# The order of work at the last output product of a mixer block, and spare TensorE products in front of the first products behind two fused norms

## The reference, cut to what matters

```python
def modulate(x, shift, scale):
    return layer_norm(x) * (1 + scale) + shift

def post_norm(x, y, gate, g, b):
    return layer_norm(ALPHA * x + gate * y) * g + b
...
xn = rms_norm(h, g_mix)
proj = xn @ w_in
```

## Time and profile before

| | |
|---|---|
| Median of 3 runs | 2158.62 us (2153.17 to 2158.88) |
| Profiled execution, its own time | 2158.39 us |
| Its span in the trace | 2156.4 us |
| TensorE matmul busy | 2076.0 us (96%) |
| VectorE, ScalarE, GpSimd busy | 1161.5, 882.7, 790.1 us |
| TensorE clock granted over the span | 0.98 |

### The profile page before, as it was taken

How to read it: one execution, slowest core, us unless ns; L and a number is a source line. 1 busy time by engine, 2 the same in 40 slices (tenths; PEclk the granted TensorE clock), 3 DMA queues, 4 the chain that set the end, 5 groups by cost and what they waited for, 6 DMA issues and landing times. The chain is left out here.

```text
span 2156.4 us, 25771 instructions
## 1 busy us (share of the span) xinstructions
PE 2076.0 (96%) x10262; PEld 1605.7 (74%) x10262; DVE 1161.5 (54%) x2012; ACT 882.7 (41%) x1391; POOL 790.1 (37%) x405
## 2 busy tenths in 40 slices
PE   6999988999999899999999999989999999999999
PEld 3877667888887767667888887677776788888866
DVE  5366748996574579964522131345997553122124
ACT  4543334443332566863322222335667432222132
POOL 0243104676563324420544444001434134444420
PEclk9999999999999799999999999999999999999999
DMA  9134611323222202112333322221111133332212
GB/s 313 59 98 156 215 59 59 98 98 117 78 97 86 79 1 79 40 59 78 108 98 98 98 98 78 79 85 40 59 59 40 59 98 108 98 98 84 97 54 98
DMA packets 186662, 194.23 MB, mean 90 GB/s; under 512 B 8496, under 2 KB 181936, under 8 KB 186160
## 3 DMA queue, kind: packets, MB, share of 16 engines
q1 hardware_dynamic: 184880, 187.35, 27.1%
q10 hardware_dynamic: 1664, 5.24, 0.7%
HBM read 190.48 MB, written 2.10 MB: 89 GB/s over the span
## 5 line engine op out<-in xcount | busy, mean ns | idle before, releaser
L2773 POOL TENSOR_TENSOR wl<-ring,wh 128x1024 fp32r<-128x1024 f32 (+1 forms) x253 | 621.3, 2460 | 908.5 <-ACT wh L1421 907.6
L1421 ACT ACTIVATE wh<-ring 128x1024 fp32r<-128x1024 f32 (+2 forms) x294 | 304.4, 1043 | 352.3 <-PE ps L796 265.2
L794 PE MATMUL ps<-xh,wh 128*128 128x512 f32 x960 | 377.0, 393 | 1.9 <-POOL wl L2773 1.7
L796 PE MATMUL ps<-xh,wl 128*128 128x512 f32 x960 | 374.3, 390 | 0.0
L795 PE MATMUL ps<-xl,wh 128*128 128x512 f32 x960 | 374.3, 390 | 0.0
L794 PE MATMUL ps<-acts,wh 128*128 128x512 f32 x880 | 348.7, 396 | 3.1 <-DVE wl L1950 3.1
L796 PE MATMUL ps<-acts,wl 128*128 128x512 f32 x880 | 350.5, 398 | 0.0
L795 PE MATMUL ps<-acts,wh 128*128 128x512 f32 x880 | 347.5, 395 | 0.0
L2415 DVE SCALAR_TENSOR_TENSOR mix<-ps,par,mix 128x441 f32<-128x441 f32 (+2 forms) x352 | 213.6, 690 | 34.0 <-ACT mix L1651 33.9
L794 PEld LDWEIGHTS ps<-xh,wh 128*128 128x128 f32 x960 | 180.6, 188 | 45.5 <-issue 7.8
L796 PEld LDWEIGHTS ps<-xh,wl 128*128 128x128 f32 x960 | 180.5, 188 | 38.0
(11 more groups left out here) (429 smaller groups left out, 3133.0 us busy)
## 6 DMA issues: line engine op xcount, KB each, us to landing
ring<-in_w_ff_dram SPq DMA_DIRECT2D x64, 1024.0 KB, 5.3
ring<-in_w_in_dram SPq DMA_DIRECT2D x28, 1024.0 KB, 5.2
ring<-in_ffn_w_up_dram SPq DMA_DIRECT2D x22, 1024.0 KB, 5.0
ring<-in_w_ada_dram SPq DMA_DIRECT2D x17, 1024.0 KB, 5.1
ring<-in_w_out_dram SPq DMA_DIRECT2D x12, 1024.0 KB, 5.3
ring<-in_ffn_w_down_dram SPq DMA_DIRECT2D x8, 1024.0 KB, 5.1
ring<-in_w_ple_gate_dram SPq DMA_DIRECT2D x8, 1024.0 KB, 5.2
early<-in_w_ada_dram SPq DMA_DIRECT2D x7, 1024.0 KB, 12.1
```

Source lines behind the costliest of these rows:

```text
L794: t.matmul(b[0:m, 0:n], s.hi[:, k, a:a + m], x2[0][:, k, :], start=k == ks[0], stop=False)
L796: i = t.matmul(b[0:m, 0:n], s.lo[:, k, a:a + m], x2[0][:, k, :], start=False, stop=k == ks[-1])
L1421: a.activation(s.hi[:, :, c], s.ap[:, :, c], ACT.Copy).then_inc(*up("hi", "hi", name, hf))
L2773: p.tensor_tensor(s.lo[:, :, c], s.ap[:, :, c], s.hi[:, :, c].bitcast(F32), ALU.subtract).then_inc(*up("lo_pool", "lo", name, hf))
```

## The change

It is made in three places. (1) At the last output product, `ahead_of_norm` on ScalarE squares rows 4 and 5, then does the high halves, then squares rows 6 and 7; before, row 6 came ahead of the high halves. This function is also used for `p2`, whose last product has no halves to do. (2) The half of weights that the plan gives to `("ug", 0, 0)` moves: ScalarE rounds it before `statistics` instead of behind it, and its low part is made by VectorE before `statistics` instead of by GpSimd behind `centered`. (3) A function `spin` issues matmuls of plain float32, 128x128 by 128x512, on constants, into a PSUM bank that the first real product starts afresh: 4 ahead of the rows behind `p1`, 7 ahead of the rows behind `p2`. Nothing reads them.

```diff
@@ tensor
+            def spin(b, n):
+
+                for i in range(n):
+                    t.matmul(b[:, :], ones, con[:, 0:512], start=True, stop=True)
+
...
                     for key in first:
-                        use(key, (key[0], 0, 0), (key[2],), who="pool")
+                        use(key, (key[0], 0, 0), (key[2],), who="vec" if key == first[0] else "pool")
                         take(key, keep=True)
+                    spin(ps(first[0]), 4)
                     for k in range(8):
                         e.wait_ge(*at("xl", "f", k))
@@ layer_mixer (called with spin as a further argument)
                         for key, w in first:
                             use(key, s.name, (0, 1), key[3] == 3, 0)
                             take(key, where=w)
+                        spin(ps(first[0][0]), 7)
                         for hf in range(2):
                             e.wait_ge(*at("lo", s.name, hf))
@@ scalar, ahead_of_norm
                 if j in (6, 7):
-                    for n in ((0, 1, 2, 3), (4, 5, 6))[j - 6]:
+                    for n in ((0, 1, 2, 3), (4, 5))[j - 6]:
                         square(tag, n, mix[:, n, :], sqf, at("shifted", tag, n))
                 if j == 7:
                     high()
+                    square(tag, 6, mix[:, 6, :], sqf, at("shifted", tag, 6))
                     square(tag, 7, mix[:, 7, :], sqf, taken(("mean", tag)))
@@ scalar
             ahead_of_norm("p1", 7, lambda: high(("wout", 7)))
+            high(("ug", 0, 0))
             statistics("p1")
-            high(("ug", 0, 0))
@@ vector
+            low(("ug", 0, 0))
             statistics("p1", True)
@@ vector, up1
-                    low(("ug", g, jl))
+                    if (g, jl) != (0, 0):
+                        low(("ug", g, jl))
```

More of the change, by code:

```diff
@@ L1166, in tensor @@
                 n = layers[l]
-                layer_mixer(e, t, l, part, product_t, turn, take, fold, spread, use)
+                layer_mixer(e, t, l, part, product_t, turn, take, fold, spread, use, spin)
                 for j in range(8):
@@ L1231, in tensor, with layer_mixer @@
                     banks.drop(("parts", "g1"))
-        def layer_mixer(e, t, l, part, product_t, turn, take, fold, spread, use):
+        def layer_mixer(e, t, l, part, product_t, turn, take, fold, spread, use, spin):
             n = layers[l]
```

## The result

The changed kernel takes 2145.5 us in the median of 5 runs (2142.68 to 2150.59), beside 2158.62 for the kernel before in 5 runs (2153.17 to 2158.94). The ratio is 0.9942 with an interval of 0.9921 to 0.9963, a gain of 12.5 us within 8.0 to 17.1. The forecast was 2143, range 2137 to 2151.

What follows compares the result with a forecast made beforehand. TensorE was taken to set the time, with waits behind `p1` and `p2`. Gains of 14.4 and 1.5 us sum to 15.9, less 0.4 for a clock fall, from 2158.4 to 2143 us; range 2137 to 2151.

Steps and rivals of the forecast that it cites:

- The sums: Sums of `p1`: with the new order, ScalarE's copy comes 3.37 us after the last product, as behind `p2`; 5.7 us gained.
- The half ahead of `statistics` at no cost: Ahead of `statistics` at `p1`: the moved half delays ScalarE's copy by 0 to 0.5 us, taken as 0; VectorE's part is covered.
- The chain of statistics: Behind `p1`, from copy to VectorE's first row: 5.43 us as behind `p2`, in place of 7.32; rows start 7.63 us earlier.
- VectorE's eight rows: Behind `p1`: 23.73 us in place of 24.71, 0.98 off one `xl` slowed beside GpSimd's half; last row at 335.77.
- the rule that the forecast weighed: VectorE's two-SBUF-input operation is blocked until a GpSimd one reading SBUF ends; in `p1` rows it would add 0.3 us gain.
- TensorE behind `p1`: The 96 matmuls keep up with VectorE at full clock and end one row after the last `xl`, at 338.56; gain 14.4 us.
- The spares behind `p1`: Four spare products end by 316.7, ahead of the first `xl` at 317.37; they cost nothing and hold TensorE's clock.
- first rival: The clock falls all the same: `p1` rows begin at half clock for 5.3 us, 3.2 us less gain, 2146.5; chance 0.17.
- second price: Same clock fall hitting the spare products too: they end at 319.0 and 719.3, rows at 343.2 and 733; 2155 us.
- The spares behind `p2`: Seven spares, 6.0 us at full clock, end 0.5 us after the first row is ready; delay absorbed, gain 1.5 us.
- The middle and the rest: From 356 to 700 us the `p1` gain is not given back; half-clock stretches elsewhere are worth 2 to 4 us either way.
- the last one: Rival at both places: spare products do nothing, the order does all, `p2` stays as it is; 2144.5 us, chance 0.05.

Runs made afterwards that it cites:

- squares alone: Kernel before with only square 6 moved behind the two high halves; the weight half stays behind `statistics` on GpSimd, no spare products: 2152.72 us, ratio 0.9986.
- change again: The changed kernel profiled and timed once more with nothing altered, against the kernel before: ratio 0.9947; its profiled run took 2147.87 us.
- spares alone: Kernel before plus 4 spare products behind `p1` and 7 behind `p2`, old order kept: 2158.19 us, ratio 0.9997.
- order alone: Changed kernel without both calls of `spin`, so both moves of order and no spare products: 2147.31 us, ratio 0.9952 against the kernel before.
- fill: Changed kernel plus 128-column spare products inside the statistics (3 and 2), with 4 and 4, 4 and 5, or no spares ahead of rows: ratios 0.9947, 0.9946, 0.9949.
- doubled spares: Changed kernel with 8 and 14 spare products in place of 4 and 7: 2156.47 us, ratio 0.9989 against the kernel before.

## Why the prediction was right, and what it had wrong

The forecast of 2143 us stands 2.5 below the median, inside its range. Point by point:

- **The sums.** Forecast: 3.37 us from the end of the product to the copy, priced by `p2`. Measured 3.37 or 3.38 in each kernel with the new order. Right, and the squares alone show that it is their order that does it.
- **The half ahead of `statistics` at no cost.** Forecast 0 to 0.5. The copy followed at 3.37 with the half and without it (squares alone). Right. VectorE's low half of 1.22 us (311.63) ended ahead of its next step at 313.59.
- **The chain of statistics.** Forecast 5.43 us from copy to first row, at full clock. The change again has 8.94 - 3.37 = 5.57, right; the first profile of the change has 9.63 - 3.37 = 6.26, since the clock fell inside the spread there. The change is not safe from that.
- **VectorE's eight rows.** Forecast 23.73; measured from 318.04 to 340.03 + 1.63 = 341.66, 23.62. Right. What is won is 24.71 - 23.62 = 1.09, where the forecast had taken 0.98 off. The third `xl` of 1.86 us is gone, and it is there again in the squares alone, which leave the half on GpSimd. By the rule that the forecast weighed (the Trainium skill, SBUF — State Buffer, "Who interferes with whom") the `xl` beside GpSimd's `centered` should be held up too. The forecast took the 0.88 us in the earlier trace rows to speak against that. It doesn't, and the traces bear the rule out for both. GpSimd and VectorE, first in the change, then in the spares alone:

```profile
324.50 1.29 POOL L2830 TENSOR_TENSOR mix<-mix,arena_f 128x512 f32<-128x512 f32 x1
```

```profile
324.09 1.27 POOL L2827 TENSOR_TENSOR mix<-mix,arena_f 128x512 f32<-128x512 f32 x1
324.34 1.57 DVE L2371 SCALAR_TENSOR_TENSOR xl<-mix,mod,xh 128x512 fp32r<-128x512 f32 x1
```

  In the change GpSimd's instruction ends at 325.79, and the `xl` of 325.54 at 326.34, 0.55 us behind it. In the spares alone the ends are 325.36 and 325.91, 0.55 again; with the half, in the earlier trace rows, 331.39 and 331.94, once more 0.55. It is so for all 29 `xl` of the thirteen profiles that start well inside a GpSimd instruction. An `xl` takes 1.86, 1.57 or 0.80 us by how much of GpSimd's instruction is still to come, and beside `centered` that happened to be little.
- **TensorE behind `p1`: the step that failed.** The forecast let TensorE end "one row after the last `xl`", 338.56 or 35.3 us after the product. Measured at full clock: 37.11 + 0.23 = 37.3, although the last `xl` ends where it was forecast (32.55 us after the product, forecast 32.53). The last two `xl` come one directly behind the other (340.03, two in 1.63 us; the same is in the earlier trace rows), so that the last row at which TensorE waits for VectorE is row 6 (it starts at 340.84), and row 7 only comes behind it. It is two rows of 2.7 us behind the last `xl` but one, not one behind the last: 2.0 us of 14.4 that the forecast's own rows could have shown. The gain there was 12.3 us in the change again and 11.7 in the first profile.
- **The spares behind `p1`.** Forecast: hidden, and holding the clock. They are hidden (they end 0.45 or 1.4 us ahead of the first `xl`), the clock stays at 1.00 in the rows, and it is worth 1.1 us rather than the 3.2 of the first rival. That rival priced the half clock by TensorE's own work over 5.3 us. It lasted 4.0 us in the rows and put the second row 2.1 us back, and about half of that was made up, since VectorE paces the rows. (With the doubled spares of its second price the four would end at 313.28 + 6.88 = 320.2 and not at 319.0; nothing hangs on it.)
- **The spares behind `p2`: mis-sized.** Forecast 6.0 us of spares ending 0.5 us behind the first row, and 1.5 us won. They took 7.38 and 7.08 us in the two profiles of the change, the first real matmul started 1.8 us behind the first `xl`, and 0.4 us was won. The working took the full clock for granted between the spread and the rows; the clock had fallen in the spread already (2.56 and 2.85 us in place of 2.05) and the first spares ran at a lowered one. With the clock up (spares alone) the result was 25.67 against 25.5 forecast. So the mechanism was right, and its condition was met in one of three profiles with 7 spares. With 4 the spares ended ahead of the data even where it wasn't met (spread of 3.13 us); with 5 no profile has it unmet.
- **The middle and the rest.** Nothing is given back between 356 and 700 us. Right: 344.87 us before and after. The 2 to 4 us either way that the forecast allowed for half-clock stretches elsewhere are there too: behind `rsT` the profiles differ by up to 6.3 us.

The sum by these terms at `p1` and `p2` is 12.75 us in the change again, beside 13.1 in the medians. That the two lie so close is partly luck, since 3.2 us are lost behind `rsT` in that profile and 1.0 won ahead of `p1`. The forecast had 15.5: 2.0 too many behind `p1`, 1.1 behind `p2`, less the 0.4 taken off. The rival nearest to what happened is the last one, that the order does all: the order alone, at 0.9952, can't be told from the change at 0.9947 in time, and in the traces the spares bring 1.1 behind `p1`. Behind `p2` the spreads of `rsT` lie 1.2 us apart (27.88 and 26.64), but 0.8 of that is the clock in the statistics ahead of the spares (VectorE's first row after 9.63 and 8.80 us), and 0.4 is theirs.

**What stays open.** Why the spread of `p2` runs at a lowered clock in some kernels is not settled. Without fill it took 2.56 to 3.68 us in six profiles of ten and 2.05 in the other four; with fill it took 2.05 in three of three. The six are all the profiles that have the half moved and no fill; the four are those with the half in its old place. So among the nine with the half moved the fill parts them cleanly, which fits a fill that helps, and would make the moved half what brings the fall. That is not shown: nine and four profiles are few, the stage lay at other times in each, and no run shows how the half would reach so far. Nor is it known why the sums of `p1` ran at half clock in two of the four profiles with the old order. No version is measurably faster than the change: the differences left are 1 us, and the runs of one kernel spread over 3 to 16 us.

## What to carry to other kernels

Ask of each chain behind a large product what its engines could have done while the product still ran: two weight halves moved ahead of a square, and one ahead of a chain, brought nearly everything here. When parts of a change are tried singly, look at the granted clock ahead of them first: by these readings 2.5 of the 5.0 us of one part, and all of the 1.2 us of another, were the clock's. When a consumer follows a producer row by row, find the last row at which it really waits, and count all its work from there; a stretch at half clock is worth only what the producer's pace does not hide. Spare products are cheap while they end ahead of the data; beyond that, seven of them cost their full 6.0 us here. So size them by their duration at half clock.

## What the runs showed of the hardware

- In some executions of either kernel the granted clock falls to 0.66 to 0.70 in 220 to 230 us, with TensorE busy for 8.9 us or more of the ten (last output product at 305.3 to 308.4 us in six of the thirteen profiles, and at 301.9 to 303.7 in the other seven). Between 200 and 300 us those six lose 3.3 to 4.9 us against the seven. In the two profiles of the changed kernel the last output product ends 6.2 us apart, half of this change's gain; stages have to be compared from a common event on.
- With the new order and 4 plain float32 products on constants ahead of them, the first rows behind `p1` ran at a granted clock of 1.00; without, after 5.0 us of idleness, at 0.50 for the first 4 us or so, behind the same statistics.
- A VectorE instruction that reads two tiles from SBUF (`xl`, 0.75 us alone) and starts while a GpSimd `tensor_tensor` of two such tiles runs ended 0.55 us behind GpSimd's, in 29 of 29 cases, whether GpSimd's instruction was one of 1.27 us (128x512) or one of 2.34 us (128x1024). The GpSimd instruction that begins while such an `xl` still runs takes 1.72 to 1.77 us in place of 1.27 (a half 2.81 in place of 2.34). VectorE's other three operations of a row, which read one tile from SBUF and one from PSUM, take 0.73 to 0.75 us beside GpSimd as well.
- Behind `p2` the clock fell inside the spread in some kernels: `rsT` was reached in 25.64 to 27.88 us (the doubled spares aside) by the same stages, depending on the spares and on where the clock fell.
